# A hybrid decoder layer on one core: head 0's query from raw residual sums, tile 1's last output quarter after tile 0's, and eight picks ranked ahead of the rest

## The reference, cut to what matters

```
h = _layernorm(ALPHA * x + mix @ w_out[l], ln1_g[l], ln1_b[l])
x = _layernorm(ALPHA * h + _peer(h, w_query[l], sub_keys[l], expert_u[l], expert_v[l]), ln2_g[l], ln2_b[l])

def _peer(h, w_query, sub_keys, expert_u, expert_v):
    q = (h @ w_query).reshape(B, S, PEER_HEADS, 2, PEER_HALF)
    s = jnp.einsum('bshcd,hckd->bshck', q, sub_keys)
    top_s, top_i = lax.top_k(s, PEER_TOPK)                       # 16 of 128, for each half
    cand = top_s[..., 0, :, None] + top_s[..., 1, None, :]       # 16 x 16 sums
    best_s, best_i = lax.top_k(cand, PEER_TOPK)
    eid = i1 * N_KEYS + i2                                       # 16 experts per head and token
    g = jax.nn.softmax(best_s, axis=-1)
    a = jax.nn.gelu(einsum('td,thkd->thk', hx, expert_u[e]))
    return einsum('thk,thkd->td', gw * a, expert_v[e])
```

## Time and profile before

| | before |
|---|---|
| median of three runs | 1811.53 us |
| the profiled execution | 1811.57 us, span 1809.8 us |
| PE busy | 1467.7 us, 81% |
| DVE busy | 1077.2 us, 60% |
| POOL busy | 752.8 us, 42% |
| ACT busy | 398.3 us, 22% |
| read from HBM | 641.47 MB, 356 GB/s over the span |
| gathers on POOL's queue | 557.62 MB, 74.8% of the DMA engines' span |

### The profile page before, as it was taken

The page is one execution under the profiler, slowest core; times in us unless marked ns, Lnnn a source line. Parts: engine busy times, 40 slices in busy tenths (PEclk is TensorE's granted clock), DMA queues, the critical chain, the costliest instruction groups (busy, mean ns, idle before and its releaser), DMA issues.

```text
span 1809.8 us, 15271 instructions
## 1 busy us (share of the span) xinstructions
PE 1467.7 (81%) x5648; PEld 866.9 (48%) x5648; DVE 1077.2 (60%) x1716; ACT 398.3 (22%) x868; POOL 752.8 (42%) x591
## 2 busy tenths in 40 slices
PE   8999999999976366787777878778877787787776
PEld 7988999987865232333333333333333333233322
DVE  6666646665699997455554545464746454544555
ACT  5665455654201030101101011010110201010200
POOL 3210000000366678455555554555555555455331
PEclk9999999999988788999999999999999999999998
...
GB/s 309 289 262 158 139 140 118 141 278 180 207 413 416 411 421 422 422 421 422 422 421 422 422 421 422 422 421 422 421 422 422 421 422 422 422 422 422 421 421 248
DMA packets 154042, 644.58 MB, mean 356 GB/s; under 512 B 11620, under 2 KB 64960, under 8 KB 87920
## 3 DMA queue, kind: packets, MB, share of 16 engines
q0 software_dynamic: 79376, 557.62, 74.8%
...
HBM read 641.47 MB, written 2.10 MB: 356 GB/s over the span
## 4 chain that ended last, share of the span: by engine, by line
DMA 55%; PE 29%; POOL 6%; DVE 5%; issue 2%; DVEq 1%; SPq 1%; ACT 1%; POOLq 0%; ACTq 0%
DMA v_slot<-in_expert_v_dram,eid 52%; PE psum_all L521 12%; PE psum_all L825 6%; PE psum_all L661 5%; POOL u_slot L467 4%; DVE u_slot L1479 3%; PE psum_all L758 2%; DMA u_slot<-in_expert_u_dram,eid 2%; POOL v_slot L482 2%; DMA w_ring<-in_w_in_dram 1%; PE psum_all L642 1%; PE psum_all L548 1%; PE psum_all L546 1%; SPq L338 0%; PE psum_all L608 0%
## 5 line engine op out<-in xcount | busy, mean ns | idle before, releaser
L825 PE MATMUL psum_all<-v_slot,diag 128*128 128x512 f32 x1920 | 890.8, 609 | 258.2 <-DMA v_slot<-in_expert_v_dram,eid 252.8
L1479 DVE SCALAR_TENSOR_TENSOR u_slot<-u_slot,xh 128x2048 f32<-128x2048 f32 x256 | 581.9, 2291 | 491.1 <-DMA u_slot<-in_expert_u_dram,eid 490.9
L825 PEld LDWEIGHTS psum_all<-v_slot,diag 128*128 128x128 f32 x1920 | 350.4, 191 | 797.7 <-DMA v_slot<-in_expert_v_dram,eid 403.9
L482 POOL DMA_INDIRECT v_slot<-in_expert_v_dram,eid x256 | 347.9, 1359 | 465.3 <-PE psum_all L825 433.1
L467 POOL DMA_INDIRECT u_slot<-in_expert_u_dram,eid x256 | 367.8, 1437 | 214.7 <-DVE eid L1472 94.2
L1088 ACT ACTIVATE diag<-ident,gate 128x128 f32<-128x128 f32 x256 | 76.4, 387 | 708.4 <-PE psum_all L825 463.2
L1155 DVE TENSOR_TENSOR w_lo<-w_ring,w_hi 128x512 fp32r<-128x512 f32 x240 | 156.9, 689 | 80.5 <-ACT w_hi L853 77.4
L521 PE MATMUL psum_all<-act_hi,w_hi 128*128 128x256 f32 x640 | 185.1, 289 | 1.1 <-DVE w_lo L1155 1.0
L521 PE MATMUL psum_all<-act_hi,w_lo 128*128 128x256 f32 x640 | 181.1, 283 | 0.0
L521 PE MATMUL psum_all<-act_lo,w_hi 128*128 128x256 f32 x640 | 181.0, 283 | 0.0
L853 ACT ACTIVATE w_hi<-w_ring 128x512 fp32r<-128x512 f32 x240 | 139.3, 622 | 44.6 <-PE psum_all L521 41.5
...
## 6 DMA issues: line engine op xcount, KB each, us to landing
...
wq_ring<-in_w_query_dram SPq DMA_DIRECT2D x32, 512.0 KB, 10.9
...
u_slot<-in_expert_u_dram,eid POOLq DMA_INDIRECT x256, 33.0
v_slot<-in_expert_v_dram,eid POOLq DMA_INDIRECT x256, 33.2
...
```

The costliest lines, as they stand in the source:

```text
L482: nc.gpsimd.indirect_dma_start(out=v_slot[m % RV][:, :], out_offset=None, in_=expert_v[0], in_offset=bass.IndirectOffsetOnAxis(ap=eid[:, n ...
L825: ins = nc.tensor.matmul(bank[(4 if n < PH else 0) + q][:, :], diag[:, n % 2, k, :], v_slot[m % RV][:, 512 * q:512 * q + 512], start=first ...
L1479: V.scalar_tensor_tensor(u_slot[m % RU][:, :], u_slot[m % RU][:, :], 1.0, xh[:, n // PH, :], ALU.mult, ALU.mult, accum_out=u_dot[:, n, k:k ...
```

## The change

The bias and the inverse root of the layer norm are taken out of the transposed activations. hT now holds the raw residual sums of a token times the gain, without mean and root, and two more columns: the gain and the bias themselves (hT is 258 columns wide). The query matmul of a head then also yields what gain and bias give. A score is the raw score, plus a product of two rows: minus the mean (with the gain's part) and the root (with the bias's part); stT holds the two statistics of each token, gb the two rows of 256 (L747 of the changed kernel). This gives the score times the root; the order of the picks is the same, and the softmax gets the inverse root as a scale.

So the first three quarters of tile 0 are transposed, evicted and multiplied into head 0's query while the fourth is still being computed. The fourth quarter is computed for tile 0 alone; tile 1's follows behind head 0's scores in 16 plain float32 matmuls (mixr holds its mixed activations joined again). After tile 0's scores of head 0, first_ids ranks only eight picks (top 8 of each half, top 8 of 64 sums), which releases the first eight gathers; the full ranking of the unit follows and gives the other eight. Query and scores are made in jobs: heads 0 and 1 for each tile apart, then both tiles of heads 2 to 7.

Buffers move: the ring of w_out is its own, query block 0 is loaded beside the third quarter, the keys and ln_g come earlier, ln_b is loaded by SP after the last item into a place that belongs to the last piece of query block 1, and that piece waits for h1_ok. h1_ok is now set after the ninth dot. Slots 2 to 6 of expert_u wait for t1_mm, the progress of tile 1's last quarter.

On PE, from the last item of the projection on: before, 32 transposes and head 0's query for tile 0 (wq_ring is the weights, ident the identity of a transpose).

The diff, cut to its core:

```diff
+HTW = SEQ + 2
+TCOL = (slice(0, P), slice(P + 2, SEQ + 2))
+JOBS = [(0, (0,)), (1, (0,)), (0, (1,)), (1, (1,))] + [(h, (0, 1)) for h in range(2, PH)]
+QBANK = (4, 2)
+SBANK = (7, 6)
...
+    hT = at("hT", [P, KC, HTW], F32, o_act)
+    mixr = at("mixr", [P, KC, P], F32, o_act + 16 * K + 128)
+    skeys = at("skeys", [P, 16, P], F32, oc + 64 * K)
+    ln_g = at("ln_g", [P, D], F32, oc + 118 * K)
+    ln_b = at("ln_b", [P, D], F32, oc + 56 * K)
+    wo_ring = at("wo_ring", [P, 4, 4, 512], F32, o_ring)
+    wq_ring = [at(f"wq_ring{i}", [P, 4, 4, 512], F32, (oc + 64 * K, oc + 32 * K)[i]) for i in range(2)]
...
+    u_home = [o_u + 16 * K, o_u + 24 * K] + [o_ring + 8 * K * i for i in range(4)] + [o_u, o_u + 8 * K]
+    v_home = [oc + 64 * K + 8 * K * i for i in range(4)] + [oc + 32 * K, oc + 40 * K] + [o_act, o_act + 8 * K]
...
+                if j == 2:
+                    sp.wait_ge(S["sk_mm"], 4)
+                    sp.wait_ge(S["y_conv"], 4)
+                    sp.wait_ge(S["norm_mm"], 8)
+                    load_wq(0, r)
+
         sp.wait_ge(S["slot_used"], N_ITEMS)
-        for q in range(4):
+        sp.dma_start(ln_b[:, :], ln1_b.partition_broadcast(P).rearrange("p a d -> p (a d)")).then_inc(S["s_lnb"], 16)
+        for q in range(3):
             load_wq(1, q)
+        sp.wait_ge(S["h1_ok"], 1)
+        load_wq(1, 3)
         for j in range(2, 4):
             for q in range(4):
                 sp.wait_ge(S["wq_used"], 4 * (j - 2) + q + 1)
                 load_wq(j, q)
...
-        pool.wait_ge(S["slot_used"], O(1, 0))
+        pool.wait_ge(S["lo_done"], C(63) + 1)
+        pool.dma_start(ln_g[:, :], ln1_g.partition_broadcast(P).rearrange("p a d -> p (a d)")).then_inc(S["s_lnrow"], 16)
+        pool.wait_ge(S["slot_used"], done(21))
         pool.dma_start(skeys[:, :, :], sub_keys[0].rearrange("h c n d -> n (h c) d")).then_inc(S["s_skeys"], 16)
-        pool.dma_start(ln_g[:, :], ln1_g.partition_broadcast(P).rearrange("p a d -> p (a d)")).then_inc(S["s_lnrow"], 16)
-        pool.dma_start(ln_b[:, :], ln1_b.partition_broadcast(P).rearrange("p a d -> p (a d)")).then_inc(S["s_lnrow"], 16)
         def gather_u(n, k):
 
             m = TOPK * n + k
             if k == 0:
-                pool.wait_ge(S["ids_ok"], n + 1)
-            if m == 6:
-                pool.wait_ge(S["h1_ok"], 1)
+                pool.wait_ge(S["ids_ok"], n + 2 if n else 1)
+            if m == 8:
+                pool.wait_ge(S["ids_ok"], 2)
+            if 2 <= m <= 6:
+                pool.wait_ge(S["t1_mm"], min(m - 1, 4))
...
-            for b in range(2):
+            for b in range(2 if j < 3 else 1):
...
+        def t1_item(i):
+
+            ins = nc.tensor.matmul(bank[1][:, :], mixr[:, i, :], wo_ring[:, i // 4, i % 4, :], start=(i == 0),
+                                   stop=(i == KC - 1))
+            if i % 4 == 3:
+                ins.then_inc(S["t1_mm"], 1)
...
+        def query_mm(n, c, k):
+
+            h, ts = JOBS[n]
+            j = h // 2
+            cols = slice(0 if 0 in ts else P + 2, SEQ + 2 if 1 in ts else P + 2)
+            if k % 4 == 0:
+                pe.wait_ge((s_wa, s_wb)[j % 2][k // 4], 32 * (j // 2 + 1))
+            ins = nc.tensor.matmul(bank[QBANK[h % 2] + c][:, cols],
+                                   wq_ring[j % 2][:, k // 4, k % 4, 256 * (h % 2) + 128 * c:256 * (h % 2) + 128 * c + 128],
+                                   hT[:, k, cols], start=(k == 0), stop=(k == KC - 1), skip_group_check=True)
+            if h % 2 and 1 in ts:
+                if c and k % 4 == 3:
+                    ins.then_inc(S["wq_used"], 1)
+            elif c and k == KC - 1:
+                ins.then_inc(S["q_mm"], 1)
+
+        def scores_of(n):
+
+            h, ts = JOBS[n]
+            b = h % 2
+            pe.wait_ge(S["qp_ok"], n + 1)
+            if 0 in ts:
+                for c in range(2):
+                    ins = nc.tensor.matmul(bank[QBANK[b] + c][0:2, 384:512], qp[:, b, c, P:P + 2], skT[:, 2 * h + c, :],
+                                           start=True, stop=True, skip_group_check=True)
+                ins.then_inc(S["gb_mm"], 1)
+            if same_bank_before(n):
+                pe.wait_ge(S["score_ok"], same_bank_before(n))
+            for t in ts:
+                for c in range(2):
+                    nc.tensor.matmul(bank[SBANK[b]][:, 256 * t + 128 * c:256 * t + 128 * c + 128], qp[:, b, c, TCOL[t]],
+                                     skT[:, 2 * h + c, :], start=(t == ts[0] and c == 0), stop=False,
+                                     skip_group_check=True)
+            pe.wait_ge(S["gb_ok"], gb_count(n))
+            pe.wait_ge(S["stT_ok"], 2 if 1 in ts else 1)
+            for t in ts:
+                ins = nc.tensor.matmul(bank[SBANK[b]][:, 256 * t:256 * t + 256], stT[0:2, t, :], gb[0:2, b, :],
+                                       start=False, stop=True, skip_group_check=True)
+            ins.then_inc(S["score_mm"], 1)
...
+                if (j, i) == (2, 5):
+                    pe.wait_ge(S["sk_ok"], 4)
+                    transpose_row(0, 0, 4, 2)
+                if (j, i) == (2, 11):
+                    pe.wait_ge(S["acc_dve"], 2 + 4 * NG + 2)
+                    transpose_row(0, 4, 8, 3)
+                if j == 3 and i in (1, 3, 5, 7):
+                    pe.wait_ge(S["hT_dve"], 1 + (i >= 5))
+                    for k in (i - 1, i):
+                        for c in range(2):
+                            query_mm(0, c, k)
+                if (j, i) == (3, 9):
+                    pe.wait_ge(S["acc_dve"], 2 + 4 * NG + 3)
+                    transpose_row(0, 8, 12, 2)
+                if j == 3 and i in (13, 15):
+                    pe.wait_ge(S["hT_dve"], 3)
+                    for k in (i - 5, i - 4):
+                        for c in range(2):
+                            query_mm(0, c, k)
...
+        t1_item(0)
+        pe.wait_ge(S["row3_ok"], 1)
+        transpose_row(0, 12, 14, 3)
+        transpose_row(0, 14, 16, 2)
+        t1_item(1)
+        for k in range(12, 16):
+            if k == 12:
+                pe.wait_ge(S["hT_act"], 1)
+            if k == 14:
+                pe.wait_ge(S["hT_dve"], 4)
+            for c in range(2):
+                query_mm(0, c, k)
+
+        def transpose_stats(t, b):
+
+            pe.wait_ge(S["std_ok"], t + 1)
+            pe.wait_ge(S["mean_ok"], t + 1)
+            nc.tensor.transpose(bank[b][0:2, 0:P], st2[:, t, :], ident[:, :]).then_inc(S["st_mm"], 1)
+
+        transpose_stats(0, 6)
+        scores_of(0)
...
+        for i in range(2, KC):
+            t1_item(i)
         for c in range(2):
             for k in range(KC):
-                query_mm(0, c, k, bank[c][:, 128:256], 1, 2)
-        for h in range(1, PH):
-            b = (h - 1) % 2
-            pe.wait_ge(S["qp_ok"], max(h, 2))
-            query_half(h, 0, b)
-            if h == 1:
-                scores_of(0, 1, 1, 2, 2)
-            else:
-                scores_of(h - 1, 1 - b, 0, 2, h + 1)
-            query_half(h, 1, b)
-        scores_of(PH - 1, (PH - 2) % 2, 0, 2, PH + 1)
+                query_mm(1, c, k)
+        scores_of(1)
+        transpose_row(1, 0, 4, 0)
+        pe.wait_ge(S["row3_ok"], 2)
+        transpose_row(1, 4, 8, 1)
+        pe.wait_ge(S["hT_act"], 2)
+        transpose_row(1, 8, 12, 0)
+        pe.wait_ge(S["hT_act"], 3)
+        transpose_row(1, 12, 16, 1)
+        pe.wait_ge(S["hT_act"], 4)
+        transpose_stats(1, 0)
+        pe.wait_ge(S["hT_act"], 5)
+        for n in range(2, len(JOBS)):
+            pe.wait_ge(S["qp_ok"], same_bank_before(n))
+            pe.wait_ge(S["gb_ok"], gb_count(same_bank_before(n) - 1))
+            for c in range(2):
+                for k in range(KC):
+                    query_mm(n, c, k)
+                if c == 0 and n > 2:
+                    scores_of(n - 1)
+        scores_of(len(JOBS) - 1)
...
+        row_out(0, 12, 14, 3, 4)
+        root_of(0)
+        query_out(0)
+        stats_out(0, 6)
+        gb_out(0)
+        score_out(0)
...
+            if h == 3:
+                act.wait_ge(S["h1_ok"], 1)
...
+        lo_to(O(1, 4))
+        out_rows(0)
+        lo_to(O(1, 8))
+        mix_raw(0, 8)
+        lo_to(O(1, 11))
+        mix_raw(8, 16)
+        V.tensor_copy(hT[:, :, P:P + 2], lncol[:, :].rearrange("p (a k) -> p k a", a=2))
+        dve.drain()
+        lo_to(O(2, 4))
+        out_rows(1)
+        lo_to(O(2, 10))
+        row_t0(0)
+        lo_to(O(3, 0))
+        row_t0(1)
+        lo_to(O(3, 4))
+        out_rows(2)
+        lo_to(O(3, 13))
+        row_t0(2)
...
+        def last_row(t):
+
+            cols = xh[:, t, 1536:2048]
+            V.scalar_tensor_tensor(cols, cols, ALPHA, bank[t][:, :], ALU.mult, ALU.add).then_inc(S["row3_ok"], 1)
+            dve.drain()
+            V.bn_stats(lnst[:, t, 3, :], cols)
+
+        def mean_of(t):
+
+            dve.drain()
+            V.bn_aggr(lnmv[:, t, :], lnst[:, t, :, :])
```

(34 more changed lines are left out.)

296 lines of the change are left out of this document (140 added, 156 removed).

## The result

The changed kernel takes 1780.09 us (median of four runs, 1779.52 to 1780.45) against 1811.41 of the kernel before: a ratio of 0.9827, interval 0.9815 to 0.984, 31.3 us less. The forecast was 1791.5 with a range of 1786 to 1801: right in sign, 11.4 us short in size, and outside the range. The profiled execution took 1780.05 us, with a span of 1778.3.

A forecast was written before the change was run, and what follows sets the result against it. From about 481 us the kernel was taken as one DMA stream of gathers, so an earlier first gather ends it earlier: 25.7 - 2.5 - 3 = 20.2 us off 1811.5, called 1791.5 us, range 1786 to 1801.

The forecast's parts named there:

- last output quarter: Output projection's last quarter, 426.6 to 448.65 us before: 14.0 us of TensorE plus 0.8 for jostling, ending at 442.3.
- From there to the scores: From the last output item to the ranking's start: 3.0 + 1.68 + 1.2, so 5.9 us, ranking at 448.2.
- Rival (c): TensorE's clock falls in the new gap, 3 us of chain work becomes 5: 1793.5; chance inside the forecast's 0.55.
- Ranking eight alone: Short ranking before the first gather: 4.0 us, bounds 3 and 5.6, against 9.1 in full; first gather at 452.6.
- More bytes: Behind the stream's start: one quarter of query block 1, 1.05 MB, now waits for h1_ok, cost 2.5 us.
- Holes in the stream: DMA gaps because only eight gathers can go at once, near 489 us: 3 us in all, bounds 1 and 6.
- Head 2: Its last weights land near 514, scores at 524; VectorE asks at 519.4 and waits some 5 us, costing nothing.
- cover of 10 us: Up to gather 55 the DMA is busy until 620 us, VectorE is there at 610, so its waits are hidden.
- (b): Last quarter doesn't shrink to 14 us, or holes and waits for heads 2 and 3 exceed 10 us: 1796 to 1801; chance 0.20.
- (a): The stream has no hole because queued gathers carry it over: 1788; with a still earlier start, chance 0.18.
- (d): Query weights come too late for the value gathers, POOL stands 40 us near 650: 1819.5, slower; chance 0.04.
- (e): No change, 1808 to 1815: earlier start, but VectorE sets the pace to gather 56; chance 0.03.

## Why the prediction was wrong

The step that failed is its last, "What gathers, products and tail do after 640 us isn't touched", repeated as "from 640 on 421 GB/s as now". No gather or product there changed, but the slots' addresses did, and that alone moved the kernel before by 18.7 us: 427 GB/s instead of 421. Nothing in the trace of before could show it, since all its slots are off alike. But the line was in the diff, and the prediction never asked what the wider hT does to the addresses behind it.

The other terms, with 18.7 taken off: the schedule gave 31.3 - 18.7 = 12.6 us where the sum had 20.2. Step by step; the last five rows compare the changed kernel with the kernel before with all slots aligned, counted from the packets of both traces at 427 GB/s:

| step | forecast | measured |
|---|---|---|
| last output quarter | 14.8 us | 17.7 us |
| its end | 442.3 | 443.96 |
| from there to the ranking | 5.9 us | 6.84 us |
| ranking eight until the first gather | 4.4 us | 4.44 us |
| first gather | 452.6 | 455.28 |
| gained at the start | 25.7 us | 22.6 us |
| more bytes behind it | -2.5 us | -3.9 us |
| DMA time not used until 640 us | -3 us | -5.5 us |
| after the last gathered row | none | -0.8 us |
| sum | 20.2 us | 12.4 us |

- **A float32 product is two rows.** This second error runs through four terms. The program of before has 24 products of head 0 behind its last transposes, and the trace 48 rows for them, in 5.38 us. The prediction took a row, 0.112 us, for a product; a product takes 0.224. (Transposes, and the matmuls of the split w_out, are one row each.) These rows of the changed kernel show it again, with 14 products of tile 1's last quarter behind the scores, then the four and the 32 products between the last weights of block 1 and head 2's scores:

```profile
450.31 12.29 PE L699 MATMUL psum_all<-wo_ring,mixr 128*128 128x512 f32 x28
...
510.45 3.81 PE L718 MATMUL psum_all<-hT,wq_ring 128*128 128x258 f32 x8 [10.05 <-DMA wq_ring<-in_w_query_dram]
...
515.67 14.22 PE L718 MATMUL psum_all<-hT,wq_ring 128*128 128x258 f32 x64
529.81 0.60 PE L734 MATMUL psum_all<-skT,qp 128*2 128x128 f32 x4
```

- **The last output quarter.** It began at 426.26, 1.2 us before the 427.5 of the forecast, and took 17.7 us instead of 14.0 + 0.8. Its 24 products cost 5.4 us and not 2.7; that is nearly all of the 2.9. The 0.8 for engines that wait for each other was about right. The run with both tiles in the quarter shows what leaving tile 1 behind is worth at the end, 9.2 us.
- **From there to the scores.** 0.9 too short. From the end of the products at 448.04 to the ranking are 2.8 us, as forecast (1.68 + 1.2). The miss lies ahead of it, 4.1 us instead of 3.0: the eight products are the sixteen rows at 446.09, 1.95 us and not 0.9. Rival (c), a fallen clock, did not happen here: the granted clock is 1.00 from 444 to 455.
- **Tile 1's products behind the scores.** Forecast done by about 455, done at 462.60, twice as long for the same reason. Nobody waited for them: POOL's next seven gathers went out with only 0.30 us of issue between them.
- **Ranking eight alone.** Right to 0.04 us in length. In worth it was wrong: about 1 us or nothing at the end and not the 4 to 5 of its length, since the holes that follow take the rest.
- **More bytes.** 1.65 MB and not 1.05. The bias row and three quarters of block 1, which should have been in by 453, were not: 321 GB/s from 444 to 455 is 3.5 of their 4.2 MB. About 1.1 us of it lies where no gathered byte moves yet.
- **Holes in the stream.** The size was off, past the bound of 6. Missing bytes against 427 GB/s: 16 x (1 - 341/427) = 3.2 us near 492 and 16 x (1 - 323/427) = 3.9 near 592, 7.1 in two dips. In all, the DMA misses 13.3 us between the first gather and 640 us, its start-up included, and 7.8 in the aligned kernel before. The first dip was forecast at 1 to 3 near 489, with at most 1 more before the weights come at 499.4; they came at 502.62. The second was not forecast. It follows from the next point.
- **Head 2.** VectorE waited 10.5 us, not 5. The weights came earlier than forecast (510.45, not 514) and VectorE asked later (522.7, not 519.4), both of which shorten the wait. But 36 products stood between the weights and the scores, 8.1 us in the forecast and 17.7 in the rows above: 16.0 for their two rows each, and 1.7 more because the first four ran at the lower clock (0.50 from 510.4 to 514.1) after TensorE's wait of 10 us for the weights. The small steps of the scores took 5.0 instead of 2. And the "cover of 10 us" that made the wait free was not there. It rested on the weights keeping the DMA busy until 620. They did not last: from 540 to 550, with POOL held for 20.46 us and the gather queue empty, SP's queue moved 3.99 MB, as this view of the two queues shows, and by 560 the weights were through. Everything behind them then had to come from slots that VectorE frees, and at 590 it had not caught up.

```profile
q1 hardware_dynamic: 2070, 3.99, 103.7%
q0 software_dynamic: 5, 0.02, 0.6%
```

- **Query weights beside gathers.** 500 to 540 ran at 406 GB/s, 2.0 us under the rate of the stream; before, 412 against 421 was 0.9. The forecast left this out; it is in the 5.5 us of the table.

So of the rivals (b) came nearest. The quarter didn't shrink to 14 us, though for its products and not because the engines waited for each other, and the two dips are 7.1 us beside a wait of 10.5 for head 2, where (b) asked for over 10. Without the addresses the time would have been 1811.4 - 12.6 = 1798.8, in its 1796 to 1801. (a), (d) and (e) did not occur, nor did (c) in its gap. A schedule that gave 7.6 less than its sum and addresses that gave 18.7 more make the 11 us by which the time lies under the forecast: two errors of opposite sign, so that the miss is smaller than the gain that was not foreseen.
